# Reciprocal roots of the norms: square root on ScalarE and reciprocal on VectorE, in a two-layer hybrid block

## What is computed

```python
def rms_norm(x, gain):
    xf = x.astype(jnp.float32)
    y = xf * lax.rsqrt(jnp.mean(xf * xf, axis=-1, keepdims=True) + EPS)
    return (y * gain.astype(jnp.float32)).astype(x.dtype)
...
for l in range(DEPTH):
    ...
    h = modulate(rms_norm(x, norm_g[l, 0]), sh1, sc1)
    x = x + 0.5 * g1[:, None, :] * swiglu(h, w_ff_in[l, 0], w_ff_out[l, 0])
    h = modulate(rms_norm(x, norm_g[l, 1]), sh2, sc2)
    x = x + g2[:, None, :] * token_mix(h, w_in[l], ...)
    h = modulate(rms_norm(x, norm_g[l, 2]), sh3, sc3)
    x = x + 0.5 * g3[:, None, :] * swiglu(h, w_ff_in[l, 1], w_ff_out[l, 1])
```

## Time and profile before

| | us |
|---|---|
| median of three runs | 1778.92 (1778.81 to 1780.08) |
| the profiled execution, its own time | 1777.92 |
| its span, first to last instruction | 1776.2 |
| PE busy | 1637.2 |
| DVE busy | 1112.1 |
| ACT busy | 807.9 |

### The profile page before, as it was taken

One profiled execution on the slowest core, in us unless ns is written; L12 is line 12 of the kernel. 1 busy time (PEld: TensorE's weight loads), 2 busy tenths in 40 slices (PEclk: granted clock), 3 DMA queues, 4 the chain that ended last, 5 costly groups with the idle time before them and its releaser, 6 DMA issues.

```text
span 1776.2 us, 29572 instructions
## 1 busy us (share of the span) xinstructions
PE 1637.2 (92%) x12873; PEld 1588.5 (89%) x12873; DVE 1112.1 (63%) x1458; ACT 807.9 (45%) x896; POOL 5.5 (0%) x23
## 2 busy tenths in 40 slices
PE   3999987888999998999999999679989999989998
PEld 3999986777999997999989999678878999989998
DVE  6676655776444886575666656467754468856444
ACT  3533435776434444443443333576654344343342
POOL 0000000000000000000000000000000000000000
PEclk7999998999998999999999999899998999999999
DMA  9888733433343994767647674334343468756552
GB/s 332 277 252 259 236 95 101 131 111 110 119 143 115 316 316 155 250 230 256 228 166 272 232 262 149 92 111 125 109 136 99 139 214 303 261 177 209 190 166 72
DMA packets 283745, 333.54 MB, mean 188 GB/s; under 512 B 13084, under 2 KB 234944, under 8 KB 283616
## 3 DMA queue, kind: packets, MB, share of 16 engines
q1 hardware_dynamic: 276816, 327.65, 56.2%
q10 hardware_dynamic: 6800, 4.00, 0.9%
HBM read 330.23 MB, written 1.38 MB: 187 GB/s over the span
## 4 chain that ended last, share of the span: by engine, by line
PE 79%; DVE 10%; ACT 8%; issue 2%; SPq 1%; DMA 0%; ACTq 0%; DVEq 0%
PE ps L451 65%; PE ps L695 3%; DVE w_lo L1116 2%; PE ps L476 2%; ACT w_hi L803 2%; PE ps L487 1%; DVE scratch L1054 1%; PE ps L729 1%; PE ps L727 1%; PE ps L734 1%; DVE scratch L1275 1%; ACT L810 1%; ACT pr L926 1%; PE ps L583 1%; ACT pr L924 1%
## 5 line engine op out<-in xcount | busy, mean ns | idle before, releaser
L451 PE MATMUL ps<-h_hi,w_hi 128*128 128x256 f32 x2464 | 716.9, 291 | 30.1 <-DVE w_lo L1116 24.7
L451 PE MATMUL ps<-h_lo,w_hi 128*128 128x256 f32 x2464 | 705.9, 286 | 0.0
L451 PE MATMUL ps<-h_hi,w_lo 128*128 128x256 f32 x2464 | 705.1, 286 | 0.0
L1116 DVE TENSOR_TENSOR w_lo<-raw,w_hi 128x2048 fp32r<-128x2048 f32 x238 | 543.5, 2286 | 175.0 <-ACT w_hi L803 174.7
L803 ACT ACTIVATE w_hi<-raw 128x2048 fp32r<-128x2048 f32 x238 | 451.9, 1907 | 205.4 <-PE ps L451 188.4
L451 PEld LDWEIGHTS ps<-h_hi,w_hi 128*128 128x128 f32 x2464 | 482.7, 196 | 37.0 <-DVE w_lo L1116 25.2
L451 PEld LDWEIGHTS ps<-h_lo,w_hi 128*128 128x128 f32 x2464 | 482.3, 196 | 2.9 <-issue 1.9
L451 PEld LDWEIGHTS ps<-h_hi,w_lo 128*128 128x128 f32 x2464 | 481.8, 196 | 0.0
L451 PE MATMUL ps<-y_hi,w_hi 128*128 128x256 f32 x704 | 201.3, 286 | 0.0
L451 PE MATMUL ps<-y_lo,w_hi 128*128 128x256 f32 x704 | 199.2, 283 | 0.0
L451 PE MATMUL ps<-y_hi,w_lo 128*128 128x256 f32 x704 | 199.1, 283 | 0.0
(11 more groups left out here) (236 smaller groups left out, 1723.4 us busy)
## 6 DMA issues: line engine op xcount, KB each, us to landing
raw<-in_w_ff_in_dram SPq DMA_DIRECT2D x176, 512.0 KB, 4.8
eyr<-in_w_ada_dram SPq DMA_DIRECT2D x144, 512.0 KB, 6.9
raw<-in_w_in_dram SPq DMA_DIRECT2D x100, 512.0 KB, 4.7
raw<-in_w_ff_out_dram SPq DMA_DIRECT2D x88, 512.0 KB, 4.7
raw<-in_w_gate_dram SPq DMA_DIRECT2D x48, 512.0 KB, 4.6
raw<-in_w_branch_dram SPq DMA_DIRECT2D x48, 512.0 KB, 4.6
raw<-in_w_out_dram SPq DMA_DIRECT2D x16, 512.0 KB, 5.6
rgw<-in_rg_w_dram ACTq DMA_DIRECT2D x16, 128.0 KB, 2.2
```

Of the source, the lines that this page charges most:

```text
L451: last = mm(outs, a, b[:, cc, :], start=not rows and cc == 0 and q == 0, stop=cc == n - 1 and q == 2, skip_group_check=True)
L1116: tt(w_lo[:, p % SPLIT, :], raw[:, p % RAW, :], w_hi[:, p % SPLIT, :].bitcast(F32), ALU.subtract).then_inc(lo_ready, 1)
```

## The change

Each of the 24 places computes a square root on ACT, which needs one activation in place of two, and a reciprocal in place on DVE, at the point where DVE is about to use `rstd`. The semaphores stay; they are now raised after the square root. A new helper `inverse` on DVE makes the reciprocal and waits for it.

```diff
@@ the first norm, ACT @@
-            steps.did(f(rstd[:, 0:T], ps[:, 4, 0:T], ACT.Ln, scale=1.0 / D, bias=eps[:, :]))
-            steps.wait()
-            f(rstd[:, 0:T], rstd[:, 0:T], ACT.Exp, scale=-0.5).then_inc(rstd_ready, 1)
+            f(rstd[:, 0:T], ps[:, 4, 0:T], ACT.Sqrt, scale=1.0 / D, bias=eps[:, :]).then_inc(rstd_ready, 1)
@@ all others, ACT; the calls rsqrt(...) become rms(...) @@
-                def rsqrt(to, sums, n, signal):
-
-                    steps.did(f(to, sums, ACT.Ln, scale=1.0 / n, bias=eps[:, :]))
-                    steps.wait()
-                    f(to, to, ACT.Exp, scale=-0.5).then_inc(signal, 1)
+                def rms(to, sums, n, signal):
+
+                    f(to, sums, ACT.Sqrt, scale=1.0 / n, bias=eps[:, :]).then_inc(signal, 1)
@@ DVE @@
+            def inverse(v):
+
+                steps.did(nc.vector.reciprocal(v, v))
+                steps.wait()
+
@@ DVE, norm @@
                     dve.wait_ge(rstd_ready, 3 * l + q + 1)
+                    inverse(rstd[:, 0:T])
@@ DVE, keys @@
                 dve.wait_ge(krs_ready, l + 1)
+                inverse(rstd[:, :])
```

More of the change, by code:

```diff
@@ L822, in norm @@
                     act.wait_ge(ss_done, 3 * l + q + 1)
-                    rsqrt(rstd[:, 0:T], ps[:, 4, 0:T], D, rstd_ready)
+                    rms(rstd[:, 0:T], ps[:, 4, 0:T], D, rstd_ready)
                 def pieces(q):
@@ L891, in _ @@
                 act.wait_ge(kss_done, l + 1)
-                rsqrt(rstd[:, :], ps[:, 2, :], HD, krs_ready)
+                rms(rstd[:, :], ps[:, 2, :], HD, krs_ready)
                 act.wait_ge(z_ready, l + 1)
@@ L917, in _ @@
                     act.wait_ge(qss_done, n + 1)
-                    rsqrt(rstd[:, :], ps[:, 2, :], HD, qrs_ready)
+                    rms(rstd[:, :], ps[:, 2, :], HD, qrs_ready)
                     hi(p + 3)
@@ L985, in _ @@
                     act.wait_ge(oss_done, n + 1)
-                    rsqrt(rstd[:, 0:T], ps[:, 4, T:2 * T], GLA_DV, ors_ready)
+                    rms(rstd[:, 0:T], ps[:, 4, T:2 * T], GLA_DV, ors_ready)
                 hi(k0 + K_L3 + 2)
```

## The result

The changed kernel takes 1791.63 us (median of four, 1791.5 to 1792.58) against 1779.29 for the kernel before (1778.81 to 1780.08): 12.3 us more, a ratio of 1.007 with a 95% interval of 1.0057 to 1.0082. The forecast was 1795, the range 1789 to 1809. The profiled execution took 1791.54 us, 13.6 more than that of before.

What follows compares the result with a forecast made beforehand. It took PE, 79% of the chain, to bound the kernel, with ACT and DVE counting where PE runs out of work. 1.79 + 2.9 + 10.9 + 0.6 = 16.2 us gave 1795 us, range 1789 to 1809.

Steps and rivals of the forecast that it cites:

- The reciprocal's size: On DVE, 153 ns plus 6.25 ns for each column: 1.75 us for 256 columns, 3.35 us for 512.
- Rival A: The reciprocal costs a third more for each column, 8.3 ns; 1809 us in all, chance 0.13.
- rival C: The reciprocal hardly grows with its columns, so the kernel gets faster: -13 us, 1766 us; chance 0.05.
- First norm: Ahead of the first block, reciprocal and wait stand on DVE's path with nothing beside them: +1.79 us.
- Five norms: At the other norms ahead of blocks, the reciprocal replaces the logarithm's table load and exponential in equal time: shift 0.
- Key norms: At two key norms, +0.16 us up to the reciprocal's reader and +1.30 for a load between Abs and Exp: +1.46 each.
- Query rounds 1 to 3: At six query norms, the reciprocal delays DVE's `lo` and the bias behind it: +1.81 us each, 10.9 in all.
- Round 0: At two query norms, DVE's `lo` ends just behind PE's scores: +0.3 us each at most, 0.6 in all.
- Gated linear attention: At eight norms in its loop, DVE's wait for PE and ACT's wait cover reciprocal and new load: shift 0.
- TensorE's clock: Over the query rounds, the granted clock of 0.92 brings no change in time; bounds +23 and -23 us.
- rival B: The clock falls further, 1.5 us more in each of eight query rounds: +12 us, 1807 us; chance 0.12.
- Rival D: A table load costs more than it shows, so removed loads return more, 1.28 us in seven places: 1786 us; chance 0.03.

Runs made afterwards that it cites:

- short_recip: The changed kernel with each of the 24 reciprocals replaced by a short multiplication by 0.01; 1764.74 us, ratio 0.9924 to the kernel before.
- first_three: The changed kernel with the first norm's reciprocal done three times over, in place; 1795.91 us, ratio 1.0095 to the kernel before.
- hidden_only: The kernel before, changed only at the five norms ahead of blocks and the eight of the gated linear attention; 1780.65 us, ratio 1.0003.
- keys_load_early: The changed kernel with a one-column exponential on ACT right behind each key norm's square root, loading the table early; 1790.5 us, ratio 1.0067 to the kernel before.
- gla_five: The changed kernel with the reciprocal in the gated linear attention's loop done five times over, in place; 1833.89 us, ratio 1.0311 to the kernel before.
- query_only: The kernel before, changed only at the eight query norms; 1791.31 us, ratio 1.0063.
- logs_early: The kernel before with one-column logarithms ahead of ACT's waits at five block norms and six query rounds; 1770.77 us, ratio 0.9949.

## Why the prediction was right, step by step

**The reciprocal's size: right.** 1.749 and 3.348 us where 1.75 and 3.35 were taken from two rows of 8 and 16 columns. Rival A (a third more for each column) is out by that row, rival C by it too; `short_recip` shows that C's total was right had the instruction been short (13.4 us measured, 13 in its sum).

**First norm, +1.79: right.** +1.79 within the timeline (42.29 - 40.50), 3.60 for two more in `first_three`, -1.63 when it is taken off the path.

**Five norms, 0: right.** From the end of the root to `hf` it is 1.89 us where it was 1.83, and `hidden_only` is within 0.2% of before.

**Key norms, +1.46 each: right.** +0.14 and +1.29 measured in the first layer, +0.20 and +1.28 in the second, and `keys_load_early` takes the 1.29 back.

**Query rounds 1 to 3, +1.81 each: right in its mechanism, 0.11 too large in its size.** All six show 1.69 to 1.71. The reciprocal starts 0.08 us before the convolution's end shows, an overlap that I had given to the `lo` and not to it.

**Round 0, +0.3 each at most: right in the sum within 0.3 us, not in the bound.** +0.65 and +0.28. The forecast had DVE's `lo` end last; in the first layer PE's scores still did, 0.42 us behind it.

**Gated linear attention, 0: right.** Flat within 0.2 us over both layers' rounds, and `gla_five` shows how much DVE time it takes until that cover is gone.

**TensorE's clock, no change: this term failed in its size,** -2.5 us in the traces in place of 0. The bounds of 23 us on either side held it. The clock itself did not change, 0.92 over the query rounds (336 to 444 us) and 0.950 against 0.949 over the span; single stretches moved by +2.41 and -1.84 us all the same. The step behind it that failed is an overlap. The prediction held, against rival B, that PE's two longer pauses about line 648 keep their length. In two of the eight rounds the one ahead of line 648 fell from 2.94 us to 1.22 and 1.25, 3.4 us in sum, since PE's slow work lay ahead of it. So the total of slow time says little: it counts only where no pause behind it takes it up. The two pauses are one item of the balance and not all of it: `query_only` has three such (1.24 to 1.26 us) at a granted clock of 0.945 over the span, and its trace is 15.4 us longer than that of before, more than its rounds' 10.3. Rival B, with +12 us, was wrong in sign as well. The forecast of 1795.1 us against 1791.6 is off by 2.6 in the traces (16.2 and 13.6) and by 0.9 where it added 1.0 us to come from a profiled execution to the median; after the change the two lie 0.1 apart.

**Rival D, more than the load shows: out.** Where a load went to or left the chain, 1.28 to 1.30 us moved (`keys_load_early`, `logs_early`). The drain that the Trainium skill adds in "ScalarE: Activation LUTs", section "What ACT_TABLE_LOAD costs", is not in these runs.

**What stays open.** Why the slow pieces of the clock fall where they do. The traces show that they fell elsewhere and what that cost or gave back; no run here chose where they fall. That they move with the start times of the work behind a pause is argued, not shown. `first_three` contradicts the one simple form of it that was tried, an end that stays in place.

## What to carry to other kernels

Price an exchange between engines by the question which of the two comes last at each site: the same edit cost nothing at thirteen places, 1.7 us at six and 1.45 at two, and what the lighter engine saved counted only where it had come last (the five norms, where it paid for the reciprocal). A table load costs its 1.28 us only where it stands behind the wait; a dummy activation of one column in the idle time ahead hides it. `logs_early`, which does so, was 8.4 us faster than the kernel before, 6.2 of them at the edited places, where a change of functions lost 12. Two short instructions of a form give its slope, and that was good to 1% here over a factor of 32 in columns, though it rested on a step of 50 ns. And a pause of an engine that another engine ends takes up lost time ahead of it: look where slow stretches lie, not only how long they are.

## What was not expected of the hardware

- The reciprocal is linear in its columns from 8 to 512: 203, 253, 1749 and 3348 ns are all 153 ns and 6.25 ns for each column within 5 ns.
- Moving a site by 1 or 2 us changes the total by less or more than that. Two saved loads of 1.29 us gave 0.8 us, two more reciprocals of 1.75 us at the start cost 4.3, and five times the reciprocals in the gated linear attention cost 42.3, of which PE's waits are about 30 and its slower rate 10.
- The same 187 matmuls took 23.34 us at a granted clock of 0.94 and 25.77 at 0.83, with the same work around them on the other engines.
- The two masks that POOL makes in a round of the gated linear attention take 0.64 us in the changed kernel, where they are done before DVE's next `lo` begins. In `gla_five` they run beside that `lo` in six of the eight rounds and take 2.62 us together, since one of them lasts up to 2.27 us in place of 0.29; in the other two rounds both take 0.65. The profile's times for POOL are rough. No engine's wait was put down to them, so it cost nothing here.
